# Three groups of score products of a chunkwise scan gathered at one place of the PE stream

## The chip, the cores and the metric

The kernel runs on one core of a Trainium2 chip. The metric is the device time of one launch in microseconds. Three runs of the kernel before took 1108.93, 1109.14 and 1109.42 us; their median is 1109.14 us.

The engines are called by short names: PE (matrix products), DVE (vector), ACT (activations, copies), POOL (a second vector engine), SP (issues most of the loads). Each runs its own list of instructions in order; semaphores tie them together.

## The reference

One inference step of a decoder trunk of two layers, for a prompt of 512 tokens and for 8 short sequences of 8 tokens (64 rows, "the sequences"). Layer 0 is an HGRN2 gated linear recurrence, layer 1 a dilated sliding-window attention. Only layer 0's mixer matters here. Cut to its core:

```
def adaln(x, c, norm_w, w_ada, b_ada):
    ada = jax.nn.silu(c) @ w_ada + b_ada
    shift, scale, gate = jnp.split(ada, 3, axis=-1)
    h = rmsnorm(x, norm_w) * (1 + scale[:, None]) + shift[:, None]
    return h, gate[:, None]

def hgrn2_mixer(h, s0, lb, w_in, b_f, g_norm_w, w_out):
    q, f, i, z = jnp.split(h @ w_in, ...)            # 8 heads: q, f 128 wide, i, z 256 wide
    q = silu(q);  f = lb + (1 - lb) * sigmoid(f + b_f);  k = 1 - f;  v = i
    o, S = hgrn2_scan(q, k, v, log(f), s0)
    return (rmsnorm(o, g_norm_w) * silu(z)) @ w_out, S

def step(S, inp):                                    # one chunk of a head
    b = jnp.cumsum(gc, axis=2)
    A[t, s] = sum_c q[t, c] * k[s, c] * exp(b[t, c] - b[s, c])      for s <= t
    o = A @ v + (q * exp(b)) @ S
    S_new = exp(b_last) * S + (k * exp(b_last - b))^T @ v
```

The chunk length is the reference's choice; the kernel works in chunks of 128 tokens.

## The kernel before, in words

**Head loop.** `pe_step`, `dve_step` and `act_step` run for h = 0 to 9. Step h projects head h (new) and scans head g = h - 1; it also ends the norm of head f = h - 2. So steps 1 to 7 do all three kinds of work, step 0 has no scan, steps 8 and 9 no new head.

**Projections.** The weights come in 512 KB pieces into three buffers, are split into a high part (ACT, L349) and a low part (DVE, L357), and PE multiplies in three passes. `project_T` (L384) makes q, f and z with tokens along the free dimension; `project_rows` (L405) makes the values v with tokens along the partitions, in four tiles of 128 prompt tokens (24 matmuls each, 128x256) and one for the sequences. The function `between` is called behind each of the four tiles; there the instruction stream of PE gets the work of head g put in between. A part of the next conditioning vector (`ada`) is made in each step 1 to 6 too: raw weight pieces of 512 KB are multiplied (L431), the sums of the step before are turned by four transposes (L463, into bank 3 of the PSUM tensor X), and DVE adds them up (L503, L495).

**Scores.** Within a chunk, exp(b[t] - b[s]) isn't formed for all pairs. For L = 1, 2, 4, ..., 64 (levels 0 to 6) the token range is cut into blocks of 2L; DVE subtracts the block's middle from b (`dve_sub`, L1041 and L1042, into dd), ACT takes the exponential (L898), and DVE multiplies it on k in the first half and q in the second (`dve_level`, L870 and L871, into qk). PE then multiplies qk with itself in 32x32 pieces (`pe_grams`): the diagonal (i = 0) and seven levels, in three groups: group 0 is i = 0, 1, 2 (60 pieces, bank 0 of X), group 1 is i = 3, 4, 5 (52 pieces, bank 1), group 2 is i = 6, 7 (16 pieces, bank 2). In the profile each such f32 matmul is two instructions. The levels of head g are made in step g, and their products are taken in step g + 1.

DVE reads the products (`dve_gram`): groups 0 and 1 by a multiplication with the identity mask (L1007) and predicated copies (L1011, mask and target in SBUF, source in PSUM), group 2 by plain copies (L1021, L1024, L1027). `dve_level(h, i)` overwrites what group (i + 1) // 3 of the step has read from qk, so it waits for `gram_ready` of that group. The next step's levels begin with the scan over tokens (L1111, which waits for ACT's logarithm L939), `dve_sub` of level 0, and so on.

**What waits behind.** POOL's two multiplications (L859, L860, both operands in SBUF) start when DVE has copied dl (L1123, L1124, behind `dve_sub` of level 1). The key transposes on PE (`pe_turn_keys`, L1237) wait for `ada_done` (L495, behind the read of group 2 on DVE). The masked keys kz (`masked_keys`, L1105) come ahead of `dve_sub` of level 5 (4 in step 7). The chunk states (`pe_chunk_states`, L1280) wait for kz and for ACT's copy kr (L948), which stands behind ACT's exponential of level 3.

Of the kernel before, what the change touches and what calls it, by code (L numbers as in the profile page):

```python
# [128 lines left out]
def program(nc, I, O):  # L129
    with ExitStack() as ctx:  # L130
# [126 lines left out]
        def ticket_w(h, t):  # L257
            return TICKETS * h + t
# [240 lines left out]
        def read_ada_chunk(chain, c):  # L499

            nc.vector.wait_ge(adt_done, c + 1)
            groups = ada_banks[c // 11].rearrange("p (m q n) -> p m n q", q=4, n=32)
            chain(nc.vector.tensor_reduce(out=adsum[:], in_=groups[:, :, 0:NC_, :], axis=AX_X, op=ALU.add))  # L503
            read_ada(c // 6, c % 6 * 4, c % 6 * 4 + 4, adsum[:])
# [544 lines left out]
        def dve_step(dve, chain, h):  # L1049
            b, g, f = h % 2, h - 1, h - 2  # L1050
            gb = g % 2
            new, scan, end = h < AH, 0 <= g < AH, 0 <= f
# [41 lines left out]
            grams = iter(range(3 if scan else 0))  # L1094

            def gram():
                for i in grams:
                    dve_gram(dve, chain, g, i)
                    break

            def masked_keys():
                dve.wait_ge(kt_ready, g + 1)
                bank, c0 = seq_keys_at(g)
                kz_in = [P, 2, ADK]
                dve.tensor_tensor(kz[:], X[:, bank, c0:c0 + P].unsqueeze(1).to_broadcast(kz_in),  # L1105
                                  seqm[:].unsqueeze(2).to_broadcast(kz_in), ALU.mult).then_inc(kz_done, 1)

            gram()
            if new:
                dve.wait_ge(g_done, h + 1)  # L1110
                dve.tensor_tensor_scan(b_[:], reset[:], fg[:], 0.0, ALU.mult, ALU.add).then_inc(b_done, 1)  # L1111
                dve.wait_ge(b_done, h + 1)
                for i in range(8):
                    if i in (0, 3):
                        gram()
                    if i == 3 and scan:
                        read_ada_chunk(chain, 3 + h)
                    if i == (5 if h < AH - 1 else 4) and scan:
                        masked_keys()
                    dve_sub(dve, h, i)  # L1120
                    if i == 1:
                        dve.wait_ge(eb_done, h + 1)
                        dve.tensor_copy(dl[:, b, 0:CH], qe[:, b, P - 1:TP:P])  # L1123
                        dve.tensor_copy(dl[:, b, CH:], qe[:, b, TP + DS - 1:T:DS]).then_inc(dl_done, 1)  # L1124
                    if i >= 1:
                        dve_level(dve, h, i - 1)
# [187 lines left out]
        def pe_step(pe, h):  # L1314
            b, g, f = h % 2, h - 1, h - 2
            new, scan, end = h < AH, 0 <= g < AH, 0 <= f
            if new and h:
                project_T(ticket_w(h, 0), ("w", h, 0))
            if end and new:
                pe_mean(pe, f)  # L1320
            if h == AH:
                out0_units(2)
                pe_mean(pe, f)
                out0_units(3)
                pe_grams(pe, g, 0)
                out0_units(4)
                pe_grams(pe, g, 1)
                pe_grams(pe, g, 2)
                out0_units(5)
                pe_turn_keys(pe, g)  # L1330
                out0_units(6)
                pe_chunk_states(pe, g)
                pe_seq_rows(pe, g)
                out0_units(7)
                pe_seq_out(pe, g)
                out0_units(8)
            if h > AH:
                out0_units(11)
                pe_mean(pe, f)
                out0_units(14)  # L1340
                pe.wait_ge(ada_done, 3 + AH)
                pe_out(pe, "out0", 1, range(8))
            if new and h:
                project_T(ticket_w(h, 1), ("w", h, 1))
            def grams(n):
                if scan:
                    pe_grams(pe, g, n)

            keys = [("w", h, 2), ("w", h, 3)]
            if new:  # L1350

                def between(tile):
                    if tile == 0:
                        grams(1)
                    if tile == 1:
                        if scan:
                            if g:
                                pe.wait_ge(fin_done, 2 * g)
                            turn_ada_groups(3 + h)
                        grams(2)  # L1360
                        wait_read(pe, ticket_w(h, 1))
                        if h < AH - 1:
                            project_ada(16 + 4 * h, 3)
                            project_ada(17 + 4 * h, 3)

                grams(0)
                project_rows(ticket_w(h, 2), keys, range(CH),
                             lambda c: PJ[:, c // 2, c % 2 * ADV:(c % 2 + 1) * ADV], between)
            if scan and new:
                pe.wait_ge(ada_done, 4 + h)  # L1370
                pe_turn_keys(pe, g)
            if new and h < AH - 1:
                project_ada(18 + 4 * h, 3)
                project_ada(19 + 4 * h, 3)
            if scan and new:
                pe_seq_rows(pe, g)
                pe_chunk_states(pe, g)
                pe_seq_out(pe, g)
            if new:
                project_rows(ticket_w(h, 3), keys, [CH], lambda c: PJ[:, 2, 0:ADV])  # L1380
                project_T(ticket_w(h, 4), ("w", h, 4))
            if scan:
                pe.wait_ge(os_done, g + 1)
                pe.wait_ge(up_read, g + 1)
                pe.wait_ge(kz_done, g + 1)
                pe_new_states(pe, g)
            if new:
                if h < AH - 1:
                    pe.wait_ge(adr_done, 5 + h)
                project_T(ticket_w(h, 5), ("w", h, 5), range(KD))  # L1390
            elif scan:
                out0_units(9)
            if scan:
                pe.wait_ge(ua_read, g + 1)
                if h == AH:
                    pe.wait_ge(at_done, 3)
                for j in range(2):
                    for c in range(CH):
                        out = X[:, 2 + j, c * P:(c + 1) * P]
                        last = pe.matmul(out, v_[:, g % 2, c, j * P:(j + 1) * P], at[:, c], start=True, stop=(c == 0))  # L1400
                        if c:
                            last = pe.matmul(out, sc[:, c - 1, j * P:(j + 1) * P], qe[:, g % 2, c * P:(c + 1) * P],  # L1402
                                             start=False, stop=True)
                last.then_inc(op_ready, 1)
# [1376 lines left out]
```

## Time and profile before

| | |
|---|---|
| median of three runs | 1109.14 us |
| profiled execution, its own time | 1108.2 us |
| span of that execution | 1106.6 us |
| PE busy | 1083.3 us, 98% |
| PE weight loads busy | 1034.7 us, 94% |
| DVE busy | 638.6 us, 58% |
| ACT busy | 508.2 us, 46% |
| POOL busy | 151.3 us, 14% |
| mean granted PE clock | 0.999 |

The span is the time from the first to the last instruction on the core. Busy shares are of the span. In the timeline, a row gives the start of an instruction (or of a run of like ones), its duration, the engine, the source line, the operation, and out<-in by the names of the tensors. Spans of neighbouring instructions overlap a little, since the tail of one runs beside the start of the next; distances from start to start add up.

### The profile page before, as it was taken

The numbers are of one execution on the slowest core, as the hardware profiler recorded it, in microseconds if no ns is written. First come the engines' busy times: TensorE is split into PE (matmuls) and PEld (weight loads), VectorE is DVE, ScalarE is ACT, GpSimd is POOL, SyncE is SP. The second block draws the span as 40 slices with busy tenths as digits, with TensorE's granted clock in tenths as the row PEclk, the third lists the DMA queues.
The fourth block names the chain that finished last, engine by engine and source line by source line (L and its number), as shares of the span: only waits on it lengthen the run. The fifth ranks groups of instructions, "written<-read, shape, count | busy, mean of one in ns | idle before, by whom it ended". The sixth has DMA issues, their size and how long they took to land.

```text
span 1106.6 us, 26211 instructions
## 1 busy us (share of the span) xinstructions
PE 1083.3 (98%) x11121; PEld 1034.7 (94%) x11121; DVE 638.6 (58%) x1282; ACT 508.2 (46%) x1041; POOL 151.3 (14%) x156
## 2 busy tenths in 40 slices
PE   8999999999999999999999999999999999999998
PEld 6799999999999998988998999999999999998997
DVE  4776767767676858773537534652464346337332
ACT  4653444444454545642225544552554356356122
POOL 1000010101000000000000720450054015300000
PEclk9999999999999999999999999999999999999999
DMA  9873545454545452219235365236522753273441
GB/s 321 289 209 96 152 131 152 134 150 131 152 131 153 125 154 79 82 60 297 77 87 171 92 163 140 81 88 149 155 62 80 159 134 86 55 160 102 138 118 44
DMA packets 232218, 147.73 MB, mean 133 GB/s; under 512 B 7875, under 2 KB 226205, under 8 KB 231590
## 3 DMA queue, kind: packets, MB, share of 16 engines
q1 hardware_dynamic: 217456, 134.17, 42.7%
q10 hardware_dynamic: 14646, 11.89, 3.2%
q8 instruction: 88, 1.44, 0.6%
q14 instruction: 28, 0.23, 0.1%
HBM read 124.00 MB, written 22.02 MB: 132 GB/s over the span
## 4 chain that ended last, share of the span: by engine, by line
PE 88%; DVE 4%; ACT 3%; DMA 2%; issue 1%; SPq 1%; ACTq 0%; DVEq 0%
PE PJ L384 27%; PE PJ L1716 18%; PE PJ L1422 14%; PE PJ L405 8%; PE X L1843 1%; PE X L1280 1%; PE X L1221 1%; PE X L1400 1%; PE X L1870 1%; PE PJ L688 1%; PE PJ L1744 1%; PE PJ L431 1%; PE X L1402 1%; DMA pre<-in_ada_w_dram 1%; PE X L1808 1%
## 5 line engine op out<-in xcount | busy, mean ns | idle before, releaser
L357 DVE TENSOR_TENSOR w_lo<-raw,w_hi 128x1024 fp32r<-128x1024 f32 (+1 forms) x128 | 157.6, 1243 | 164.7 <-ACT w_hi L349 163.7
L349 ACT ACTIVATE w_hi<-raw 128x1024 fp32r<-128x1024 f32 (+1 forms) x128 | 129.3, 1025 | 161.4 <-PE PJ L1716 69.3
L1716 PE MATMUL PJ<-w_hi,h_hi 128*128 128x256 f32 x600 | 167.3, 287 | 0.9 <-DVE w_lo L357 0.7
L1716 PE MATMUL PJ<-w_lo,h_hi 128*128 128x256 f32 x600 | 164.6, 283 | 0.0
L384 PE MATMUL PJ<-h_hi,w_hi 128*128 128x288 f32 (+1 forms) x736 | 160.7, 300 | 0.6 <-ACT v_ L944 0.6
L384 PE MATMUL PJ<-h_hi,w_lo 128*128 128x288 f32 (+1 forms) x736 | 157.6, 296 | 0.0
L384 PE MATMUL PJ<-h_lo,w_hi 128*128 128x288 f32 (+1 forms) x736 | 157.4, 295 | 0.0
L1716 PE MATMUL PJ<-w_hi,h_lo 128*128 128x256 f32 x480 | 135.8, 283 | 0.0
L384 PEld LDWEIGHTS PJ<-h_hi,w_hi 128*128 128x128 f32 x736 | 118.1, 189 | 4.6 <-issue 3.1
L384 PEld LDWEIGHTS PJ<-h_hi,w_lo 128*128 128x128 f32 x736 | 118.9, 189 | 0.0
L384 PEld LDWEIGHTS PJ<-h_lo,w_hi 128*128 128x128 f32 x736 | 118.8, 189 | 0.0
L1716 PEld LDWEIGHTS PJ<-w_hi,h_hi 128*128 128x128 f32 x600 | 115.0, 192 | 1.7 <-DVE w_lo L357 0.9
L1716 PEld LDWEIGHTS PJ<-w_lo,h_hi 128*128 128x128 f32 x600 | 115.1, 192 | 0.0
L1422 PE MATMUL PJ<-oz_low,w_hi 128*128 128x256 f32 x448 | 96.1, 296 | 0.0
L1716 PEld LDWEIGHTS PJ<-w_hi,h_lo 128*128 128x128 f32 x480 | 92.1, 192 | 0.0
L405 PE MATMUL PJ<-w_hi,h_hi 128*128 128x256 f32 x320 | 91.1, 292 | 0.8 <-DVE q_ L1067 0.8
L405 PE MATMUL PJ<-w_lo,h_hi 128*128 128x256 f32 x320 | 88.1, 283 | 0.0
L1422 PEld LDWEIGHTS PJ<-oz_low,w_hi 128*128 128x128 f32 x448 | 75.6, 190 | 0.0
L405 PE MATMUL PJ<-w_hi,h_lo 128*128 128x256 f32 x256 | 72.4, 283 | 0.0
L898 ACT ACTIVATE dd<-dd 128x576 f32<-128x576 f32 (+1 forms) x64 | 41.4, 657 | 62.7 <-DVE dd L1042 53.2
L405 PEld LDWEIGHTS PJ<-w_hi,h_hi 128*128 128x128 f32 x320 | 61.2, 191 | 3.3 <-issue 1.6
L1189 DVE SCALAR_TENSOR_TENSOR xT<-PJ,ada,xT 128x128 f32<-128x128 f32 (+1 forms) x40 | 17.8, 499 | 75.5 <-PE PJ L1422 75.5
(347 smaller groups left out, 2145.4 us busy)
## 6 DMA issues: line engine op xcount, KB each, us to landing
raw<-in_a_w_in_dram SPq DMA_DIRECT2D x48, 512.0 KB, 4.9
raw<-in_b_w_in_dram SPq DMA_DIRECT2D x64, 256.0 KB, 3.9
raw<-in_ada_w_dram SPq DMA_DIRECT2D x28, 512.0 KB, 3.9
kvc<-in_cache_kv_w_dram SPq DMA_DIRECT2D x24, 512.0 KB, 5.7
pre<-in_ada_w_dram SPq DMA_DIRECT2D x16, 512.0 KB, 9.9
s<-in_state_hgrn_dram SPq DMA_DIRECT2D x8, 1024.0 KB, 8.2
out_hgrn_sample_dram<-s ACTq DMA_DIRECT2D x8, 1024.0 KB, 5.1
raw<-in_a_w_out_dram SPq DMA_DIRECT2D x16, 512.0 KB, 5.1
```

Of the source, the lines that this page charges most:

```text
L349: act.activation(w_hi[:, i % SPLITS, 0:size], raw[:, n % RAWS, 0:size], ACT.Copy).then_inc(hi_done, 1)
L357: dve.tensor_tensor(w_lo[:, i % SPLITS, 0:size], raw[:, n % RAWS, 0:size], w_hi[:, i % SPLITS, 0:size].bitcast(F32), ALU.subtract).then_in ...
L384: last = nc.tensor.matmul(PJ[:, 2 * s + e, 0:n1 - n0], a[:, k, :], b[:, k, n0:n1], start=(k == 0 and i == 0), stop=(k == KD - 1 and i == 2))
L405: last = nc.tensor.matmul(out_of(tile), a, b[:, k % 4, :], start=(k == 0 and i == 0), stop=(k == KD - 1 and i == len(passes) - 1))
L431: last = nc.tensor.matmul(PJ[q:q + 32, bank, n % 4 * P:n % 4 * P + P], scT[:, k, :], w[:, k, :], start=(k < 4), stop=(k >= 4))
L688: last = pe.matmul(PJ[:, 2 * t + e, 0:HT], a[:, k, :], b[:, k, e * HT:(e + 1) * HT], start=(k == 0 and i == 0), stop=(k == KD - 1 and i == 2))
L898: act.activation(dd[:, x % 2, 0:n], dd[:, x % 2, 0:n], ACT.Exp).then_inc(exp_done, 1)
L1189: dve.scalar_tensor_tensor(out=x, in0=y, scalar=gate, in1=x, op0=ALU.mult, op1=ALU.add)
L1221: last = pe.matmul(gram_at(i)[BL * q:BL * q + BL, n], left[:, t:t + BL], right[:, t:t + BL], start=True, stop=True)
L1280: last = pe.matmul(X[:, c // 2, c % 2 * ADV:(c % 2 + 1) * ADV], kr[:, c], v_[:, g % 2, c], start=True, stop=True)
L1422: last = pe.matmul(PJ[:, 2 * (t % 2) + e, 0:z - x], a[:, n % nk, :], b[:, x:z], start=(n == 0 and i == 0), stop=(n == 2 * nk - 1 and i == 2))
L1716: last = pe.matmul(PJ[:, tile // 2, tile % 2 * 256:tile % 2 * 256 + 256], a, b[:, k, :], start=(first and k == 0 and i == 0), stop=(kk == ...
```

## The change

In steps 1 to 7, PE's three score groups are no longer spread over three places (ahead of the first tile of the value rows, behind the first, behind the second) but stand in a row behind the second tile, behind the four transposes of the conditioning sums. DVE's reads of group 0 and 1 move: group 0 from ahead of the scan to ahead of level 1's subtraction, group 1 from behind the scan to ahead of level 2's, group 2 stays ahead of level 3's. Steps 0, 8 and 9 are as they were.

```
             grams = iter(range(3 if scan else 0))      # dve_step; gram() reads the next group
...
-            gram()
+            if not new:
+                gram()
             if new:
                 dve.wait_ge(g_done, h + 1)
                 dve.tensor_tensor_scan(b_[:], reset[:], fg[:], 0.0, ALU.mult, ALU.add).then_inc(b_done, 1)
                 dve.wait_ge(b_done, h + 1)
                 for i in range(8):
-                    if i in (0, 3):
+                    if 1 <= i <= 3:
                         gram()
                     if i == 3 and scan:
                         read_ada_chunk(chain, 3 + h)
...
                 def between(tile):                     # pe_step
-                    if tile == 0:
-                        grams(1)
                     if tile == 1:
                         if scan:
                             if g:
                                 pe.wait_ge(fin_done, 2 * g)
                             turn_ada_groups(3 + h)
-                        grams(2)
+                        for group in range(3):
+                            grams(group)
                         wait_read(pe, ticket_w(h, 1))
                         if h < AH - 1:
                             project_ada(16 + 4 * h, 3)
                             project_ada(17 + 4 * h, 3)
 
-                grams(0)
                 project_rows(ticket_w(h, 2), keys, range(CH),
                              lambda c: PJ[:, c // 2, c % 2 * ADV:(c % 2 + 1) * ADV], between)
```

On PE, at the end of the second projection of step 1 (L384) and the start of the value rows (L405); a bracket names the semaphores that an instruction waits for:

```order
 L384 MATMUL PJ<-h_lo,w_hi 128x288 x2
 L384 MATMUL PJ<-h_hi,w_lo 128x288 x2
-L1221 MATMUL X<-q_,k_ 32x32 [waits lv_done,pj_read0,k_done]
-L1221 MATMUL X<-q_,k_ 32x32 x19
-L1221 MATMUL X<-qk 32x32 [waits lv_done]
-L1221 MATMUL X<-qk 32x32 x19
-L1221 MATMUL X<-qk 32x32 [waits lv_done]
-L1221 MATMUL X<-qk 32x32 x19
 L405 MATMUL PJ<-w_hi,h_hi 128x256 [waits raw_split,pj_read0]
 L405 MATMUL PJ<-w_hi,h_lo 128x256
```

Group 0 has left this place; group 1 leaves the one behind the first tile in the same way.

On PE, behind the second tile of the value rows in the same step (L1221 and L1227 of before are L1222 and L1228 of the changed kernel):

```order
 L463 MATMUL X<-ident,adr 128x128 x4
-L1227 MATMUL X<-qk 32x32 x8
-L1227 MATMUL X<-qk 32x64 x8
+L1222 MATMUL X<-q_,k_ 32x32 x20
+L1222 MATMUL X<-qk 32x32 x92
+L1228 MATMUL X<-qk 32x32 x8
+L1228 MATMUL X<-qk 32x64 x8
 L431 MATMUL PJ<-raw,scT 32x128 x16
```

All 128 score products now stand between the transposes and the conditioning product.

On DVE, the same step before, from the keys k_ on:

```order
L1093 TENSOR_SCALAR k_<-fg 128x576
L1007 TENSOR_TENSOR atd<-X,eye 128x160
L1011 COPY_PREDICATED atd<-lev,X 128x160 x2
L1111 SCALAR_TENSOR_TENSOR b_<-reset,fg 128x576
L1011 COPY_PREDICATED atd<-lev,X 128x160
L1011 COPY_PREDICATED atd<-lev,X 128x128 x2
L1041 TENSOR_TENSOR dd<-b_ 128x288
L1042 TENSOR_TENSOR dd<-b_ 128x288
L1041 TENSOR_TENSOR dd<-b_ 128x144x2
L1042 TENSOR_TENSOR dd<-b_ 128x144x2
```

And there now:

```order
L1112 SCALAR_TENSOR_TENSOR b_<-reset,fg 128x576
L1041 TENSOR_TENSOR dd<-b_ 128x288
L1042 TENSOR_TENSOR dd<-b_ 128x288
L1007 TENSOR_TENSOR atd<-X,eye 128x160
L1011 COPY_PREDICATED atd<-lev,X 128x160 x2
L1041 TENSOR_TENSOR dd<-b_ 128x144x2
L1042 TENSOR_TENSOR dd<-b_ 128x144x2
L1124 COPY dl<-qe 128x4
L1125 COPY dl<-qe 128x8
L870 TENSOR_TENSOR qk<-k_,dd 128x288
L871 TENSOR_TENSOR qk<-q_,dd 128x288
L1011 COPY_PREDICATED atd<-lev,X 128x160
```

The read of group 0 (L1007 and two L1011) has moved behind the first pair of subtractions, and the read of group 1 (three L1011) behind the first pair of products (L870, L871).

## Rows read from the trace of the kernel before

**Rows 1.** The page, chain that ended last, shares by engine:
```profile
PE 88%; DVE 4%; ACT 3%; DMA 2%; issue 1%; SPq 1%; ACTq 0%; DVEq 0%
```

**Rows 2.** Busy time in step 4 (us, instructions), granted clock, DMA share, GB/s:
```profile
259.00:313.55 54.55, 54.55 (x725) 51.65 (x728) 38.69 (x85) 25.78 (x36) 3.72 (x3) 1.00 0.46 139
```

**Rows 3.** PE in step 4: start, duration, engine, line, operation; last, L1221 by source:
```profile
258.53 0.43 PE L384 MATMUL PJ<-h_hi,w_lo 128*128 128x288 f32 x2
...
263.12 1.10 PE L1221 MATMUL X<-qk 128*32 128x32 f32 x104
264.15 0.39 PE L405 MATMUL PJ<-w_hi,h_hi 128*128 128x256 f32 x1
264.37 0.28 PE L405 MATMUL PJ<-w_hi,h_lo 128*128 128x256 f32 x1
...
267.13 0.60 PE L463 MATMUL X<-ident,adr 128*128 128x128 f32 x4
267.66 0.83 PE L1227 MATMUL X<-qk 128*32 128x32 f32 x30
268.28 0.30 PE L431 MATMUL PJ<-raw,scT 128*32 128x128 f32 x1
...
275.20 0.60 PE L1237 MATMUL X<-ident,kh 128*128 128x128 f32 x4
...
278.13 1.13 PE L1280 MATMUL X<-v_,kr 128*128 128x256 f32 x4
...
L1221 PE MATMUL X<-qk x1472: 196/196/217, 95.6 to 470.4; 128*32 128x32 f32 x184
```

**Rows 4.** Timeline of DVE in step 4:
```profile
262.92 0.32 DVE L1007 TENSOR_TENSOR atd<-X,eye 128x160 f32<-128x160 f32 x1
...
264.02 1.36 DVE L1111 TENSOR_TENSOR_SCAN b_<-reset,fg 128x576 f32<-128x576 f32 x1
265.41 1.01 DVE L1011 COPY_PREDICATED atd<-lev,X 128x160 f32<-128x160 uint8 x3
266.46 0.46 DVE L1041 TENSOR_TENSOR dd<-b_ 128x288 f32<-128x288 f32 x1
...
267.21 0.47 DVE L1041 TENSOR_TENSOR dd<-b_ 128x288 f32<-128x288 f32 x1
...
268.95 0.46 DVE L1041 TENSOR_TENSOR dd<-b_ 128x288 f32<-128x288 f32 x1
269.33 1.54 DVE L1042 TENSOR_TENSOR dd<-b_ 128x288 f32<-128x288 f32 x1
270.80 0.45 DVE L870 TENSOR_TENSOR qk<-k_,dd 128x288 f32<-128x288 f32 x1
...
271.53 0.91 DVE L1021 COPY at<-atd 32x128 f32<-32x128 f32 x4
...
274.20 0.20 DVE L495 TENSOR_TENSOR ada<-adsum,params 128x36 f32<-128x36 f32 x1
...
277.19 0.42 DVE L1105 TENSOR_TENSOR kz<-X,seqm 128x256 f32<-128x256 f32 x1
```

**Rows 5.** Timeline of POOL in step 4:
```profile
269.06 1.50 POOL L860 TENSOR_TENSOR qe<-qe,q_ 128x512 f32<-128x512 f32 x1
```

**Rows 6.** Timeline of DVE (step 4, attention) and POOL (attention):
```profile
286.28 0.40 DVE L422 TENSOR_TENSOR v_<-v_low,PJ 64x256 f32<-64x256 f32 x1
...
613.74 0.40 DVE L422 TENSOR_TENSOR oz<-oz,X 64x256 f32<-64x256 f32 x1
...
612.69 1.71 POOL L1702 TENSOR_TENSOR ra<-rb,tsin 128x256 f32<-128x256 f32 x1
```

**Rows 7.** Timeline of DVE and PE in step 7; in brackets idle time before:
```profile
437.85 0.20 DVE L495 TENSOR_TENSOR ada<-adsum,params 128x36 f32<-128x36 f32 x1
...
438.10 0.66 PE L1237 MATMUL X<-ident,kh 128*128 128x128 f32 x4
...
440.87 1.32 PE L1280 MATMUL X<-v_,kr 128*128 128x256 f32 x5 [0.59 <-ACT kr L948]
```

More of the change, by code:

```diff
@@ L1106, in masked_keys @@
                                   seqm[:].unsqueeze(2).to_broadcast(kz_in), ALU.mult).then_inc(kz_done, 1)
-            gram()
+            if not new:
+                gram()
             if new:
@@ L1113, in dve_step @@
                 for i in range(8):
-                    if i in (0, 3):
+                    if 1 <= i <= 3:
                         gram()
@@ L1352, in between @@
                 def between(tile):
-                    if tile == 0:
-                        grams(1)
                     if tile == 1:
@@ L1359, in between @@
                             turn_ada_groups(3 + h)
-                        grams(2)
+                        for group in range(3):
+                            grams(group)
                         wait_read(pe, ticket_w(h, 1))
@@ L1364, in between @@
                             project_ada(17 + 4 * h, 3)
-                grams(0)
                 project_rows(ticket_w(h, 2), keys, range(CH),
```

## The prediction

> **What bounds the kernel now.** I read the chain of waits first. The reader is to see that 88% of the span hangs on PE, the rest of the engines together holding a tenth [rows 1]. Then busy time by stretches: step 4 of the head loop, from 259.00 to 313.55 us, has PE busy for all of its 54.55 us, DVE for 38.69, ACT for 25.78, at a granted clock of 1.00 [rows 2]; the steps before and after repeat it to 0.05 us. So a shorter PE stream shortens the run, microsecond for microsecond, as long as no other engine becomes late; and any moment in which PE waits for DVE is added in full. The question is therefore two numbers per step: what PE saves, and how far DVE slides back relative to the two places where PE needs it. DVE's slack there has to be read off start times, since DVE's busy share (71%) says nothing of it.
>
> The change acts in steps 1 to 7 only (step 0 has no previous head, steps 8 and 9 no new one). All times below are those of step 4.
>
> **PE: what is saved.** PE's stream goes from the last L384 pair (258.53) to the first L431 matmul of the conditioning product (268.28): 9.75 us [rows 3]. In it stand three score groups with a row tile between each two. What a visit costs beyond its matmuls: the first tile matmul after a group starts 0.22 us before the second (264.15, 264.37), where the later ones are 0.12 apart: 0.10. A group of 104 matmuls of 32x32 lasts 1.10, its last one alone 0.20, so 0.90 of issue; but from its start to the next tile matmul are 1.03 (263.12 to 264.15): 0.13. What the sum below saves beyond these two lies in the way in. A tile is 2.98 with the slow first matmul (264.15 to 267.13), so 2.88 without. New stream: last L384 pair 0.27 (two of 288 columns at the pace of 0.12 per 256), two tiles of 2.88 = 5.76, four transposes up to the first score matmul 0.53 (267.13 to 267.66), group 0 of 120 matmuls 0.90 x 120/104 = 1.04, group 1 0.90, group 2 0.62 (267.66 to 268.28). Sum 9.12, so PE saves 0.63 us a step, two visits at about 0.31. Work and weights are the same; no DMA is moved, and PE passes no wait that is not long met at the new place (DVE splits the tiles' weights, L357, ahead of the step's norm work, one projection earlier).
>
> The Trainium skill (TensorEngine Tiling (Array Packing), Key Properties) says that a change of tiling mode drains TensorE. The rows agree with a price of 0.31 us for a way in and out. By that rule alone the run would be 7 x 0.63 = 4.4 us shorter; what stands against it is the other engine, which the rule doesn't speak of.
>
> **DVE: what is moved.** Group 0 is now read behind sub 0 (L1041, L1042 of level 0), not ahead of the scan; group 1 behind level 0's products, not behind the scan; group 2 stays where it is. No work is added. I follow when each can start [rows 4].
> Scan and sub 0: the scan started at 264.02 with group 0's read ahead of it; now it can't start later, and with 1.39 for itself (264.02 to 265.41) and 0.75 for sub 0 (266.46 to 267.21) DVE is free by 266.16.
> Group 0: PE comes to it at 258.53 + 0.27 + 5.76 + 0.53 = 265.09; its last matmul ends 1.04 + 0.20 later, 266.33. So DVE waits, which it did not do before: it starts at 266.37 (hand-over 0.04). Queued behind are sub 1, and behind that the copies that let POOL start and ACT's exponential of level 1. Reading takes 1.10 (262.92 to 264.02), so sub 1 starts at 267.47 where it was 267.21: 0.25 late.
> Group 1 and POOL: POOL's multiplication of 128x512 (L860) began at 269.06 and ended at 270.56 [rows 5]. Beside it L1042 of sub 2 took 1.54 where the same form beside no POOL takes 0.45: it started at 269.33 and was really done as if begun at 270.42 (the next instruction starts at 270.80, 0.38 later). So DVE lost 1.08 to POOL, and POOL ran 1.23 after the port came free at 269.33. In the new order the instructions that DVE has beside L860 are the three predicated copies of group 1, one operand of which lies in PSUM. Do they stand still too? L860 falls only in this place, but in the attention stage there is a pair of the kind: a POOL multiplication from 612.69 for 1.71 us, and in it DVE's L422, one operand in PSUM, 0.40 us; the same form with POOL idle takes 0.40 as well [rows 6]. So I take the copies at their 1.05 (265.41 to 266.46), and let POOL run beside them. They begin about 269.1 and end before 270.2. POOL now begins at 269.06 + 0.25 = 269.31 and doesn't wait, so it ends at 269.31 + 1.23 to 1.28 = 270.54 to 270.59, and DVE resumes 0.14 ahead of that, about 270.42: sub 2 is held 0.3, not 1.08. Its two instructions take 0.75, so level 1's products start at 271.17 against 270.80. DVE is 0.37 late from there on, with the same instructions as before behind. Bounds: at 0.05, if POOL holds nothing any more (sub 2 at 270.10); at 1.25, if the copies are held like the subtractions (0.25, and the full 1.05 of group 1 now behind sub 1, less the 0.05 that overlaps). I take 0.37, near the row of L422.
>
> The Trainium skill (SBUF — State Buffer, section on its two separate sides) says that a DVE operation with two SBUF inputs and a GpSimd one that reads SBUF exclude each other for a whole instruction. The 1.54 and the 0.40 both agree. The page doesn't say whether the destination that a predicated copy keeps counts as an input; if it does, the upper bound holds.
>
> **Where PE meets DVE.** First the transposes of the keys (L1237), which wait for the conditioning sum (L495). That ended at 274.40; with 0.37 it is 274.77, and PE can start at 274.82 (in step 7 PE starts 0.05 behind L495's end of 438.05, so the hand-over is 0.05 [rows 7]). PE would like to start at 275.20 - 0.63 = 274.57. So 0.25 of the saving is waited away here. Then the chunk states (L1280), which wait for the masked keys kz (L1105). Those ended at 277.61, now 277.98, so PE can start at 278.03; PE itself comes there at 274.82 + 2.93 (275.20 to 278.13) = 277.75 and waits 0.28 more. Before it started at 278.13. What is left of 0.63 is 0.10 us.
> Behind L1280 the chain of the step is PE's again: ACT's copies of the row outputs and DVE's sc follow PE, and the next steps' waits of DVE are for ACT, which waits for PE. So 0.10 stays.
>
> Step 7 is other: it has no conditioning product between, and PE already waited there. L1237 began at 438.10, right behind L495 (437.85 + 0.20), and L1280 at 440.87, after 0.59 idle for ACT's kr, which stands behind an exponential of DVE's sub 3 [rows 7]. Both slide with DVE: 0.37 longer.
>
> **Sum.** Six steps at -0.10 are -0.6, step 7 is +0.37: -0.2 us. The profiled execution's own time is 1108.2 (span 1106.6, so 1.6 lie around it), which makes 1108.0; it lies 0.9 below the median of the runs, 1109.14, and the same 0.2 off that gives 1108.9.
>
> **Rivals.**
> (a) The port held by POOL is gone altogether, or DVE gets to its places 0.3 earlier than I reckon. For it: PE's saving is real, and the copies beside POOL use 1.05 of its 1.23. Against it: L860 can't end before 270.5 if it starts 0.25 later and lasts 1.23. Then DVE is 0.05 late, kz ends at 277.66, L1280 starts at 277.71: -0.42 x 6 + 0.05 = -2.5, giving 1106.7.
> (b) Slower: the predicated copies are held by POOL as the subtractions were. One mechanism at one place, 1.25 late: kz ends 278.86, L1280 starts at 278.91, +0.78 a step, x 6 = 4.7, and step 7 +1.25: +5.9, giving 1115.1. For it: the two inputs and the output of the copies, of which two are in SBUF. Against it: L422 has the same places for its operands. It turns slower than before from a DVE delay of 0.47 on (where L1280 is back at 278.13).
> (c) The change doesn't give what it says on PE: the groups behind one another at one place cost what they cost apart, for instance since a group's matmuls don't follow the one before at once. PE then reaches the end of group 0 no earlier by much (say 266.6), DVE is 0.3 later than in the forecast, 0.67: +0.20 x 6 + 0.67 = +1.9, giving 1111.0. Against it: group 2 starts directly behind four transposes in today's stream with no more than 0.53.
>
> **How the numbers follow.** The forecast's case 0.55 (its own range 1107.3 to 1110.8, DVE's delay 0.1 to 0.65), (a) 0.18, (b) 0.15, (c) 0.12. A change below 0.2% (2.2 us: 1106.9 to 1111.4) can't be told from none here. (a) lies at the edge of it, and the forecast's lower tail too: faster 0.20. (b) and a part of (c) are slower: 0.24. Same 0.56. The range for 8 in 10 goes from 1106.0, which takes in (a), to 1113.0, which leaves out (b) and a little at the lower end.
>
> **What the changed kernel's profile would show.** Right: in step 4's like, tile matmuls directly behind L384, 48 of them 0.12 apart; DVE idle 0.2 to 0.3 ahead of the first read of scores, with PE's score matmuls as releaser; the predicated copies of group 1 still 0.34 each beside L860, and the 1.54 of L1042 gone, the first instruction of sub 2 lengthened by 0.3 instead; PE waiting about 0.25 ahead of the key transposes and 0.28 ahead of the chunk states. Wrong: copies of over 0.5 us each (then b); no wait of PE at either place (a); score matmuls of over 1.3 us for group 0 (c). The forecast also fails if DVE's delay doesn't stay the same from level 1 to kz, since both meeting places rest on it.

## The result, and the profile after

The changed kernel is slower. It takes 1124.66 us (median of 4 runs, 1123.36 to 1126.70) against 1109.28 us for the kernel before (4 runs, 1108.93 to 1111.08): ratio 1.0137, 95% interval 1.0122 to 1.0151, or 15.4 us more. The forecast was 1108.9 us, 0.2 less than before, with a range up to 1113.0, so it was wrong in sign and in size. The profiled execution took 1123.36 us with a span of 1121.7, which is 15.1 above the span of before.

The page of the changed kernel: busy time by engine, one DMA queue (packets, MB, share of 16 engines), and the chain of waits by engine, which answers to [rows 1].

```profile
PE 1083.0 (97%) x11121; PEld 1036.1 (92%) x11121; DVE 633.7 (56%) x1282; ACT 508.8 (45%) x1041; POOL 148.2 (13%) x156
...
q8 instruction: 88, 1.44, 0.5%
...
PE 89%; DVE 3%; issue 2%; ACT 2%; DMA 2%; SPq 1%; ACTq 0%; DVEq 0%
```

PE is busy for as long as before (1083.0 against 1083.3 us), with as many instructions. So the time is idle time of PE. What it waited for stands in the waits of PE from 90 to 480 us (line waited at, releaser: us in total, times, longest):

```profile
PE X L1222 <- issue: 8.7, 5, 2.1
PE X L1228 <- issue: 3.8, 2, 2.0
PE PJ L405 <- issue: 2.3, 2, 1.6
PE PJ L431 <- issue: 1.1, 1, 1.1
```

These are 15.9 us, and none of it is a wait for DVE, ACT or a transfer. "Issue" means that the profile shows nothing that the engine waited for. In steps 1 to 7 of the kernel before, PE has no such gap. The gap of step 4 is in PE's rows (start, us, engine, line, operation, out<-in, count, idle before), which answer to [rows 3]:

```profile
272.15 0.60 PE L463 MATMUL X<-ident,adr 128*128 128x128 f32 x4
272.68 0.53 PE L1222 MATMUL X<-q_,k_ 128*32 128x32 f32 x38
...
273.07 1.74 PE L1222 MATMUL X<-qk 128*32 128x32 f32 x182
274.65 0.64 PE L1228 MATMUL X<-qk 128*32 128x32 f32 x24
277.28 0.36 PE L1228 MATMUL X<-qk 128*32 128x64 f32 x6 [1.99 <-issue]
277.44 0.30 PE L431 MATMUL PJ<-raw,scT 128*32 128x128 f32 x2
...
285.86 0.60 PE L1238 MATMUL X<-ident,kh 128*128 128x128 f32 x4
```

Step 4 begins at 266.60 here (ACT's first sigmoid; 259.00 before). The scores begin 6.08 us into the step, where 6.09 was forecast, and run at the forecast pace up to 275.1. Then, inside group 2, with its operands long there, PE stands still for 1.99 us. The same happens in each of the seven steps, once or twice, at places that mostly differ, in the scores or just behind them.

DVE and POOL in step 4, which answer to [rows 4] and [rows 5]:

```profile
273.11 0.45 DVE L1042 TENSOR_TENSOR dd<-b_ 128x288 f32<-128x288 f32 x1
273.95 0.32 DVE L1007 TENSOR_TENSOR atd<-X,eye 128x160 f32<-128x160 f32 x1 [0.39 <-PE X L1222]
...
276.82 1.00 DVE L1011 COPY_PREDICATED atd<-lev,X 128x160 f32<-128x160 uint8 x3
277.86 0.49 DVE L1041 TENSOR_TENSOR dd<-b_ 128x288 f32<-128x288 f32 x1
278.27 0.44 DVE L1042 TENSOR_TENSOR dd<-b_ 128x288 f32<-128x288 f32 x1
...
282.05 0.20 DVE L495 TENSOR_TENSOR ada<-adsum,params 128x36 f32<-128x36 f32 x1
```

```profile
276.12 0.46 POOL L859 TENSOR_TENSOR qz<-qe,q_ 128x64 f32<-128x64 f32 x1 [18.73 <-DVE dl L1125]
276.54 1.49 POOL L860 TENSOR_TENSOR qe<-qe,q_ 128x512 f32<-128x512 f32 x1
```

DVE does what was forecast: it reads group 0 at 7.35 into the step (forecast 7.37), its three copies beside L860 take 1.00, the 1.54 of L1042 is gone, and L495 starts 15.45 in (forecast 15.57 with this step's numbers). PE comes to the key transposes 19.26 in, 3.8 us behind DVE, so the two meeting places don't matter any more.

A second effect is in the stretches right behind the gap of step 4 (window, length, then busy us and count of PE, PEld, DVE, ACT, POOL; granted clock, DMA share, GB/s), which answer to [rows 2]:

```profile
277.60:281.60 4.00, 4.00 (x49) 3.62 (x40) 3.86 (x14) 0.68 (x1) 0.43 (x1) 0.58 0.54 149
281.60:285.60 4.00, 4.00 (x35) 4.00 (x34) 3.41 (x11) 0.63 (x1) 0.00 (x0) 0.99 0.96 289
```

For 3.4 us (278.2 to 281.6) the granted clock is at its lower level, 1.2 instead of 2.4 GHz, after PE has stood still for 2 us. Step 3 has the same (220.2 to 223.6). There the way from L431 to the key transposes takes 8.44 and 8.42 us, where it takes 6.92 in steps 1 and 6 and in the kernel before: 1.5 us each.

In the steps with one gap the sum closes. Take the distance from record to record at the gap (table below), less 0.63 of saving as forecast, plus 1.5 where the clock was low: that is 1.35, 3.20, 3.08 and 1.50 us for steps 1, 3, 4 and 6, and these steps last 1.31, 3.18, 3.06 and 1.53 us longer than before. Over steps 1 to 7 the ten gaps come to 18.1 us from record to record (15.9 of them idle, the rest is the tail of the product ahead), the clock to 3.0 and the saving to 4.4. That makes 16.7, of which 15.1 show in the span; some 0.9 of the difference lie in step 7, and the rest isn't assigned.

**Where the gaps lie.** The next table counts PE's records in the trace of the changed kernel, one by one in the order of time and from 0: weight loads, matmuls, and the 335 semaphore and drain instructions between them. The record number is that of the first record behind the gap. A score product in full precision is four of them (two loads, two matmuls), so the 128 products of a step are 512. The gaps are those of over 0.9 us from record to record in steps 1 to 7.

```
step  gap from  length  record number  number mod 256  records since the step's first score
1     103.76    1.98     1985          193             477
2     158.85    2.03     3265          193             313
2     162.97    1.35     3521          193             569 (behind the scores)
3     216.70    2.31     4801          193             405
4     275.07    2.21     6337          193             497
5     331.74    1.92     7617          193             333
5     336.45    0.92     7873          193             589 (behind the scores)
6     388.78    2.13     9153          193             425
7     444.15    1.31    10433          193             261
7     447.21    1.92    10689          193             517 (behind the scores)
```

All ten gaps stand at a multiple of 256 plus 193, though their places in the scores differ. The queue "q8 instruction" of the page moved 88 packets of 16 KB (1.44 MB / 88), and PE has 22,577 records: 256.6 per packet. Three kernels below change the count of records, and the packets follow. So PE's instructions come from memory in blocks of 256, and PE stands still where one block ends and the next isn't there. PE runs through 256 score records in 1.11 us (4.3 ns each). In none of the traces of this case did two packets of q8 start nearer to one another than 3.29 us, and in the long run of experiment 8 they are 3.45 to 4.1 apart. Near the gap of step 4 a packet starts at 274.72 and PE goes on at 277.28, 2.6 us later; near the other gaps it is 2.3 to 2.6.

The same counts tell how far ahead the instructions are. The block ends are at records 193, 449 and so on; let them and the packets of q8 both be numbered from 0. Packet k starts when PE is about at block end k: in the changed kernel 68 of the 88 start less than 50 records from it, and in none of the traces does one start more than 37 records ahead of it. PE passes block end k + 1 in none of the traces sooner than 2.16 us behind the start of packet k. By these counts one block is in hand, and no more. At the ten gaps the packet starts 0.04 to 1.16 us behind the block end before, and PE goes on 2.3 to 2.6 us after that, but PE needs only 1.1 to 2.8 us for the 256 records between the two block ends; the rest is the gap (step 4: 1.02 + 2.56 - 1.37 = 2.21). In steps 1 to 7 of the kernel before, 256 records with scores in them have tiles in between, and most such stretches take 4.0 to 5.3 us.

The Trainium skill (Runtime: NRT & Kernel Launch, Instruction fetch mechanics) says that the instruction memory is refilled in blocks of 16 KiB, 256 instructions, and that crossing a block's end is "mostly hidden", since the sequencers issue slower than blocks come in. The block size agrees with the trace (16 KB, 256.6 records). That it is hidden holds for tile matmuls, and not for these score products; the measurement decides.

The kernel before shows the beginning of it too. In its step 8, which the change leaves alone, groups 1 and 2 (272 records) already follow one another directly, and group 0 (240 records) stands only six larger matmuls ahead of them. These are its rows:

```profile
467.76 0.85 PE L1221 MATMUL X<-qk 128*32 128x32 f32 x78
468.54 0.53 PE L1422 MATMUL PJ<-h_hi,w_hi 128*128 128x256 f32 x2
...
469.52 1.10 PE L1221 MATMUL X<-qk 128*32 128x32 f32 x104
470.47 0.32 PE L1227 MATMUL X<-qk 128*32 128x32 f32 x9
471.52 0.71 PE L1227 MATMUL X<-qk 128*32 128x32 f32 x23 [0.73 <-issue]
```

The gap of 0.73 is at record 11,713, again a multiple of 256 plus 193. The prediction did not look at step 8.

### The profile page after: what moved, and what is told of

Read it like the earlier page. It is cut to its first block, busy times and chain, and to the rows that moved or that the text cites. A ratio compares the mean times of both kernels' runs of the same rounds, so it can differ in the third digit from the quotient of the medians.

```text
span 1121.7 us, 26211 instructions
## 1 busy us (share of the span) xinstructions
PE 1083.0 (97%) x11121; PEld 1036.1 (92%) x11121; DVE 633.7 (56%) x1282; ACT 508.8 (45%) x1041; POOL 148.2 (13%) x156
## 3 DMA queue, kind: packets, MB, share of 16 engines
q8 instruction: 88, 1.44, 0.5%
## 4 chain that ended last, share of the span: by engine, by line
PE 89%; DVE 3%; issue 2%; ACT 2%; DMA 2%; SPq 1%; ACTq 0%; DVEq 0%
PE PJ L384 26%; PE PJ L1715 18%; PE PJ L1421 14%; PE PJ L405 9%; PE X L1222 2%; PE X L1842 1%; PE X L1281 1%; PE X L1399 1%; PE PJ L431 1%; PE X L1869 1%; PE PJ L688 1%; PE PJ L1743 1%; PE X L1401 1%; DMA pre<-in_ada_w_dram 1%; PE X L1807 1%
## 5 line engine op out<-in xcount | busy, mean ns | idle before, releaser
L384 PE MATMUL PJ<-h_hi,w_hi 128*128 128x288 f32 (+1 forms) x736 | 160.7, 300 | 0.6 <-ACT v_ L944 0.6
L384 PE MATMUL PJ<-h_hi,w_lo 128*128 128x288 f32 (+1 forms) x736 | 157.7, 296 | 0.0
L384 PE MATMUL PJ<-h_lo,w_hi 128*128 128x288 f32 (+1 forms) x736 | 157.4, 296 | 0.0
L384 PEld LDWEIGHTS PJ<-h_hi,w_hi 128*128 128x128 f32 x736 | 118.1, 189 | 4.6 <-issue 3.1
L384 PEld LDWEIGHTS PJ<-h_hi,w_lo 128*128 128x128 f32 x736 | 119.0, 189 | 0.0
L384 PEld LDWEIGHTS PJ<-h_lo,w_hi 128*128 128x128 f32 x736 | 118.8, 189 | 0.0
L1715 PEld LDWEIGHTS PJ<-w_lo,h_hi 128*128 128x128 f32 x600 | 115.1, 192 | 0.0
L405 PE MATMUL PJ<-w_hi,h_hi 128*128 128x256 f32 x320 | 90.9, 292 | 0.8 <-DVE q_ L1067 0.8
L405 PE MATMUL PJ<-w_lo,h_hi 128*128 128x256 f32 x320 | 89.1, 286 | 0.6 <-issue 0.6
L405 PE MATMUL PJ<-w_hi,h_lo 128*128 128x256 f32 x256 | 73.4, 287 | 1.6 <-issue 1.6
L405 PEld LDWEIGHTS PJ<-w_hi,h_hi 128*128 128x128 f32 x320 | 62.5, 195 | 3.8 <-issue 2.7
L405 PEld LDWEIGHTS PJ<-w_lo,h_hi 128*128 128x128 f32 x320 | 62.3, 195 | 1.7 <-issue 1.7
```

The costliest lines, as they stand in the source:

```text
L384: last = nc.tensor.matmul(PJ[:, 2 * s + e, 0:n1 - n0], a[:, k, :], b[:, k, n0:n1], start=(k == 0 and i == 0), stop=(k == KD - 1 and i == 2))
L405: last = nc.tensor.matmul(out_of(tile), a, b[:, k % 4, :], start=(k == 0 and i == 0), stop=(k == KD - 1 and i == len(passes) - 1))
L1715: last = pe.matmul(PJ[:, tile // 2, tile % 2 * 256:tile % 2 * 256 + 256], a, b[:, k, :], start=(first and k == 0 and i == 0), stop=(kk == ...
```

## Experiments

The theory to be tested, called S (supply) here: PE ran out of instructions, because 512 short ones stand in a row. Its rivals: the reading order of DVE costs (D), and what costs is that the groups follow one another at that place, by their data or banks, whatever the count of instructions (P, place).

**1. DVE's order alone.** PE as before, DVE as changed:

```
-            gram()
+            if not new:
+                gram()
...
-                    if i in (0, 3):
+                    if 1 <= i <= 3:
                         gram()
```

> DVE reads the score groups in the changed kernel's order, PE's stream is the one of before. Theory S (instruction supply: PE runs out of fetched instructions in the long run of 512 score records, which come in blocks of 256): PE's stream is untouched, so within 0.3% of before, 1107 to 1112 us, and no idle PE of over 0.5 us in steps 1 to 6. Rival D (the loss is DVE's: the late reads hold back the conditioning sum, the masked keys and kr): most of the 15 us must show, over 1117 us.

Measured: 1109.65 us (12 runs, 1107.63 to 1111.63), ratio 0.9996 (0.9985 to 1.0008). Steps 1 to 6 last 54.55 us as before (the first 54.66), and PE has no gap in steps 1 to 7 (in step 8, where before has 0.73, it has 1.2). L495 starts 14.99 into step 4, 0.21 earlier than before. D falls: the order on DVE costs nothing by itself.

**2. The same kernel, 128 records later.** The warm-up matmuls at the kernel's start are 32 more, which shifts every later record by 128; the work of the steps is that of the changed kernel:

```
-        WARM = 12
+        WARM = 12 + 32
```

> The changed kernel with 32 more warm-up matmuls on PE at its very start (128 instruction records), where PE waits anyway. Theory S: 1120 to 1130 us, and each long gap moves by half a block: in step 1 it lies behind some 352 of the 512 score records in place of 480, and again all long gaps fall at one remainder of the record number by 256. Rival P (the run of small products itself stalls after so many of them, in PSUM or in the array, or DVE's reads of X disturb PE's writes): the gap stays where it is in the program, behind 480 records in step 1.

Measured: 1128.32 us (4 runs), ratio 1.0170 (1.0151 to 1.0189). The warm-ups cost 4.6 us at the start (step 1 begins at 100.12, not 95.54). The gap of step 1 moved. First the changed kernel's PE rows of step 1, then this kernel's:

```profile
101.63 0.53 PE L1222 MATMUL X<-q_,k_ 128*32 128x32 f32 x38
...
103.57 0.39 PE L1228 MATMUL X<-qk 128*32 128x32 f32 x13
105.74 0.59 PE L1228 MATMUL X<-qk 128*32 128x32 f32 x16 [1.78 <-issue]
```

```profile
106.21 0.53 PE L1222 MATMUL X<-q_,k_ 128*32 128x32 f32 x38
...
106.59 1.32 PE L1222 MATMUL X<-qk 128*32 128x32 f32 x132
110.12 0.60 PE L1222 MATMUL X<-qk 128*32 128x32 f32 x48 [2.20 <-issue]
```

From 477 records behind the first score it went to 349, so 128 earlier, into group 1. All nine gaps of over 0.9 us in its steps 1 to 7 (1985, 3521, 4801, 5057, 6337, 7873, 9153, 9409, 10,689) are again 193 above a multiple of 256. A wait for data or a bank would have stayed at its product, and a stall after so many products would have stayed at 477. P falls; S stands.

**3 and 4. Half the instructions.** The operands of the score products are taken as the upper 16 bits of each value (bf16), in the kernel before and in the changed one; the low parts are left out of the scores. A product is then one load and one matmul, and the packets of q8 are 80 instead of 88.

```
+        def high(ap):
+            return ap.bitcast(mybir.dt.bfloat16)[:, 1::2]
...
-    last = pe.matmul(gram_at(i)[...], left[:, t:t + BL], right[:, t:t + BL], ...)
+    last = pe.matmul(gram_at(i)[...], high(left[:, t:t + BL]), high(right[:, t:t + BL]), ...)
```

> The kernel before with the score products taken of the high halves of k, q and qk as bf16, so the scores lose their low bits. Each product is then 2 records (weights, matmul) in place of 4. Both theories: PE saves about half of the groups' issue, at most 1.3 us a step, 9 us in all: 1100 to 1109 us.

> The changed kernel with the same bf16 score products (scores without their low bits): 256 records in a row in each step in place of 512. Theory S: the long gaps go or shrink to under 1 us in most steps, and the kernel is -3 to +5 us against the bf16 kernel in the order of before. Rivals D and P: the distance to that kernel stays near the 15 us of the f32 pair (D: DVE's order is the same; P: the number of products is the same).

Measured: 1106.11 us (10 runs) for the order of before, ratio 0.9967 (0.9956 to 0.9979); 1104.50 us (4 runs) for the changed order, ratio 0.9955 (0.9937 to 0.9972). With half the score instructions, the change that cost 15.4 us costs none: the two medians differ by 1.6 us in its favour (0.9 in the profiled spans). The changed order's PE in step 4, and its waits:

```profile
264.34 0.30 PE L1226 MATMUL X<-q_,k_ 128*32 128x32 bf16 x20
264.48 0.95 PE L1226 MATMUL X<-qk 128*32 128x32 bf16 x92
...
265.51 1.07 PE L431 MATMUL PJ<-raw,scT 128*32 128x128 f32 x32
...
273.52 0.66 PE L1242 MATMUL X<-ident,kh 128*128 128x128 f32 x4 [0.99 <-DVE ada L495]
...
276.93 1.32 PE L1285 MATMUL X<-v_,kr 128*128 128x256 f32 x5 [0.35 <-DVE kz L1105]
```

```profile
PE X L1242 <- DVE ada L495: 5.4, 6, 1.0
PE X L1285 <- DVE kz L1105: 1.8, 5, 0.4
PE PJ L431 <- issue: 1.6, 1, 1.6
```

Here the meeting places of the forecast are real: PE waits for L495 and for kz in nearly each step. The gaps of issue are down from 15.9 us to 1.6 in step 2 and 1.1 behind the scores elsewhere (256 score records instead of 512). So the prediction's picture of DVE and PE holds where the supply costs little.

**5. Two visits instead of three.** Group 0 goes back ahead of the first tile, groups 1 and 2 stay together behind the second: 272 records in a row. DVE as in the change.

```
-                        for group in range(3):
+                        for group in range(1, 3):
                             grams(group)
...
+                grams(0)
                 project_rows(...)
```

> PE takes group 0 ahead of the first tile as before, groups 1 and 2 behind the second; DVE reads in the changed kernel's order. 272 score records in a row, 352 with the transposes and the conditioning product around them, in some 2.3 us. Theory S: one visit less saves 0.31 us a step (2 us), and gaps come only where two block boundaries fall into those 352 records, in 2 or 3 of 7 steps at 1 to 2 us: 1108 to 1114 us, a third or less of the change's 15 us. A loss that grows with the number of products at one place would be near half of it, 1116.

Measured: 1110.65 us (12 runs, 1107.92 to 1111.94), ratio 1.0001 (0.9989 to 1.0012). Steps 3 and 4 last 54.26 us, 0.29 below before, which is one visit saved (forecast: 0.31 each). The gaps in steps 1, 2 and 5 (0.21, 1.03, 0.44 us), and one of 1.3 in step 8, take it back. The time lies in the range expected under S, the gaps are shorter than the 1 to 2 us given there, and a loss that grows with the number of products at one place (1116) is excluded. In step 4 a run of 272 comes through without a gap:

```profile
267.39 1.10 PE L1222 MATMUL X<-qk 128*32 128x32 f32 x104
268.34 0.80 PE L1228 MATMUL X<-qk 128*32 128x32 f32 x30
268.94 0.30 PE L431 MATMUL PJ<-raw,scT 128*32 128x128 f32 x1
```

**6. Two visits at another pair of places.** As many visits and the same DVE order as in experiment 5, but the pair in a row is the long one: groups 0 and 1, 448 records, behind the first tile, and group 2 behind the second.

```
 def between(tile):
+                    if tile == 0:
+                        grams(0)
+                        grams(1)
                     if tile == 1:
...
+                        grams(2)
```

> Two visits again, but groups 0 and 1 together behind the first tile (448 records in a row, in 1.9 us), group 2 behind the second. DVE's order is the changed kernel's, as in the kernel with two visits that had 272 in a row and came out even. Theory S, with a block of 256 records coming every 3.5 us at the least: two boundaries fall into the 448 in about three steps of four, the second 1.1 us behind the first, so a gap of some 2.4 us there: 7 x 0.75 x 2.4 = 12.6, less 2 for the visit: 1116 to 1123 us, gaps all at the same remainder. If the number of visits or the total of records counted, it would be even with before.

Measured: 1125.27 us (4 runs, 1123.82 to 1126.72), ratio 1.0130 (1.0110 to 1.0151): slower than I expected, 1116 to 1123, and as slow as the whole change. Its waits of PE from 90 to 490 us, step 8's 1.0 among them:

```profile
PE X L1222 <- issue: 9.2, 5, 2.9
PE PJ L405 <- issue: 4.4, 2, 2.7
PE X L1228 <- issue: 1.0, 1, 1.0
```

Between experiments 5 and 6 the visits and DVE's order are the same; what differs is the length of the longest run, 272 or 448 records. That decides some 14 us (ratios 1.0130 and 1.0001). The gaps are longer here than in the change (2.44, 2.70, 2.89 in three of the steps), which S as I had put it did not give. In these three the packet starts 1.4, 2.7 and 1.9 us behind the block end before, where it was 1.2 at most in the change. The granted clock, too, is at its lower level in three pieces in these steps, about 1.5 us each.

**7. More score instructions at the old places.** The kernel before, with group 1 issued a second time behind the first tile (the surplus one comes first; `False` keeps it from signalling that the group is ready):

```
                     if tile == 0:
+                        if scan:
+                            pe_grams(pe, g, 1, False)
                         grams(1)
```

> The kernel before, with group 1's products issued twice in a row (same results written again): 208 records more in each of steps 1 to 7, at one place 416. Plain issue costs 0.90 us a step, 6.3 us in all: 1115.5 us if nothing else comes. Theory S: gaps at block boundaries come on top, 0.5 to 2 us a step, 1118 to 1130 us, though neither DVE's order nor the place of any group is changed.

Measured: 1133.24 us (4 runs, 1129.62 to 1136.66), ratio 1.0210 (1.0188 to 1.0233), 23.7 us more and above the 1118 to 1130 that I expected. At its pace on PE (0.90 us for 104 matmuls) a second group 1 costs 0.9 a step, 6.3 in seven. The rest is 13.1 us of idle PE at block ends in steps 1 to 7, and three pieces of 3.4 us at the lower clock. PE's rows of step 5 as an example:

```profile
329.51 1.65 PE L1221 MATMUL X<-qk 128*32 128x32 f32 x171
334.39 0.75 PE L1221 MATMUL X<-qk 128*32 128x32 f32 x37 [3.23 <-issue]
```

Nothing was moved here and DVE has its old order, so the gaps come with the longer row of instructions. Step 6 has none although its row is as long: there the packet starts 0.45 us behind the block end and PE needs 2.96 us for the 256 records, and it gets through. The packets of q8 rise to 94, as its 24,033 records ask for (256 x 94 = 24,064).

**8. A long run by itself.** The kernel before with 400 products of 32x32 at its end, of constant data, waiting for nothing:

```
+            for n in range(400):
+                q = n % 4
+                pe.matmul(X[BL * q:BL * q + BL, 0, 0:BL], ones[:, 0:BL], ones[:, BL:2 * BL], start=True, stop=True)
```

> The kernel before with 400 f32 32x32 matmuls (1600 records) on PE behind everything else. Theory S: after the first one or two blocks they run at 3.0 to 3.7 us per 256 records, with gaps at the block boundaries, 19 to 22 us in all. Without a limit of supply they go at 2.2 us per 256 matmul records in 512 (1.1 us per 256 records), 7 us in all.

Measured (one run): 1128.28 us. PE's rows:

```profile
1105.64 2.02 PE L2755 MATMUL X<-ones 128*32 128x32 f32 x201 [0.97 <-ACT yr L2513]
1110.11 1.31 PE L2755 MATMUL X<-ones 128*32 128x32 f32 x128 [2.45 <-issue]
1113.86 1.93 PE L2755 MATMUL X<-ones 128*32 128x32 f32 x128 [2.44 <-issue]
1117.33 1.94 PE L2755 MATMUL X<-ones 128*32 128x32 f32 x128 [1.54 <-issue]
1121.08 1.93 PE L2755 MATMUL X<-ones 128*32 128x32 f32 x128 [1.81 <-issue]
1124.82 1.40 PE L2755 MATMUL X<-ones 128*32 128x32 f32 x87 [1.81 <-issue]
```

After a head of 201 matmuls, PE runs in rows of exactly 128 matmuls, 256 records with their loads, which start 3.75, 3.47, 3.75 and 3.74 us apart, each 2.3 to 2.6 us behind the start of a packet on q8 (1107.69, 1111.24, 1115.02, 1118.47, 1122.56). That is the supply by itself: about 14 ns per record, where these products use 4.3 at the full clock. The run of 400 takes 20.6 us, in the 19 to 22 expected; without a limit 7 were expected. The clock was at its lower level from the third row on, and the distances didn't grow, so it is not PE that sets them.

**9. Two visits, conditioning later.** Experiment 5 with the conditioning product (64 records) moved behind the third tile, which leaves 272 records with nothing short beside them:

```
+                    if tile == 2:
                         wait_read(pe, ticket_w(h, 1))
                         if h < AH - 1:
                             project_ada(...)
```

> As the kernel with two visits, and the first half of the conditioning product (64 records) stands behind the third tile in place of right behind the scores: 288 records in a row. Theory S: at most one step in four has a gap, under 1.5 us; 1107 to 1111 us, no slower than the kernel with two visits. If only the score products counted it would be the same as that.

Measured: 1111.82 us (11 runs, 1108.93 to 1112.22), ratio 1.0013 (1.0003 to 1.0023). Steps 1 to 7 have no gap of issue any more, but steps 1 to 6 last 54.6 to 55.45 us: the product is a visit of its own again, and its weight piece is given back later, so that step 3 waits 0.53 for the next one to land. The time is 0.8 above the range that I expected, and the kernel is no faster than that of experiment 5, but 1.2 us slower. No version in full precision beats the kernel before.

## Why the prediction was wrong

**The step that failed: PE's stream.** The prediction took 0.90 us per 104 matmuls at constant pace for all three groups and summed 9.12 us. The pace was right as long as instructions were there (0.90 a group; the first score at 6.08 to 6.09, forecast 6.09). But L431 begins 10.58 to 10.94 us into steps 1 to 6, where 9.28 (268.28 less 259.00) less 0.63 = 8.65 was forecast: 1.9 to 2.3 late, by gaps of 1.7 to 2.1 us (idle time). The sum had no term for the supply of instructions and gave no reason for leaving it at nothing. What the runs show in its place are ten gaps with 15.9 us of idle PE; supply by itself gives 256 records per 3.5 to 3.75 us, where the sum let PE run through them in 1.1. "PE passes no wait that is not long met" left out the one wait that no semaphore carries. Experiments 2, 3 and 4, 6, 7 and 8 show this cause; experiment 8 measures it.

**The gain was real.** One visit saved gave 0.29 a step in experiment 5 (forecast 0.31), and steps 1, 3, 4 and 6 of the change close to 0.04 us with 0.63 each.

**DVE's steps were right.** Wait ahead of group 0: 0.39 where 0.2 to 0.3 was said, start at 7.35 (7.37). Copies beside POOL 1.00 for three, not held: rival (b) falls. Of the 1.08 lost to POOL nothing to speak of is left (0.49 and 0.44 for the pair of sub 2; I had left 0.3). L495 at 15.44 to 15.80 in seven steps (15.57).

**The meeting places** were right as a mechanism and are seen in experiments 3 and 4. In the changed kernel PE comes so late (17.5 to 19.4 us in, where it would have been 15.6) that neither wait occurs, and so nothing of DVE's is on the path. The prediction named "no wait of PE at either place" as the sign of its faster rival (a); the sign is there, and the reason is the opposite one.

**Rival (c)** said that groups in a row might cost more, "since a group's matmuls don't follow the one before at once". That is the nearest to what happened, but it had 0.12 of the chance and a price of 1.9 us, because it limited the loss to the visits' saving and to DVE. Its argument against, that group 2 follows four transposes directly, looks at 64 records, which a block covers. The rows of step 8 would have pointed at it: 0.73 us of idle PE, put down to "issue", in 512 records with only six larger matmuls among them, which is nearly what the change makes of each of steps 1 to 7.

**The clock** was taken at 1.00 throughout. 3.0 us of the loss are half-clock pieces that came right behind two of the gaps. The four timed runs differ by 3.3 us with mean granted clocks of 0.992 to 0.997 (the slowest has the lowest), so the pieces come and go between runs. Why these two gaps and not the others stays open. They are the longest of the ten (2.31 and 2.21 us), but length doesn't decide it: in experiment 2 the clock stays up behind a gap of 2.54 and falls behind one of 2.25.

That a gap is 1.0 us here and 3.2 there for runs of like length comes from when the packet starts and how long PE has work up to the block end. Open is why a packet starts 0.04 us behind a block end in one place and 2.7 in another. Whether the fetches wait for other transfers wasn't tried.

## What to carry to other kernels

Count TensorE's instructions in a row, loads and matmuls, and compare them with what is fetched: here 256 per 3.5 to 3.75 us. Tile matmuls stay far below that (one and its load in 0.12 us, so 256 records in 15 us); 32x32 products in full precision ask for three times as much, so it pays to keep them in pieces of less than 256 records with larger work between (240, 208 and 64 in the kernel before; the 256 in a row of experiment 4 still had a gap of 1.6 us once). Idle time put down to "issue" at constant distances in the instruction count is the sign of it, and one such gap in an untouched stage of the profile is the warning.

## What the runs showed of the hardware

- TensorE's instructions come over an own DMA queue in packets of 16 KB, 256 instructions each (88 packets for 22,577; 94 for 24,033; 80 with bf16 scores). Packets started never less than 3.29 us apart in the traces of this case. They started at most 37 records ahead of the block end that they belong to by count, so one block of 256 was in hand. A starved PE went on 2.3 to 2.6 us after a packet's start in the changed kernel, and 2.2 to 3.0 in all traces.
- An f32 product of 32x32 is four instructions at 4.3 ns each, the same in bf16 two. Bf16 scores made the kernel before 0.33% faster (experiment 3), at the cost of their low bits.
- Behind a gap of 2 us the granted clock fell to 1.2 GHz for 3.4 us in two of seven steps, 1.5 us each.
- A predicated copy with its source in PSUM takes 0.33 us beside a GpSimd multiplication, no more than alone, while DVE's subtraction with all operands in SBUF took 1.54 instead of 0.45 there.
